# A hybrid encoder step on one core: small matmuls in another order, a rotary sum moved by DMA, decays put into copies, first weights in pieces

## What is computed

```python
hn = rmsnorm(x)
qa,ka,va,ga | qb,kb,vb,gb,low | qc,kc,vc = hn @ W_in
A = retention(rotary(qa), rotary(ka) * 1/8, va)      # 4 heads, chunks of 64, scalar decay gamma_h
B = gla(qb * 1/8, kb, vb, log_f(low))                # 4 heads, chunks of 64, decay per element
C = band_attention(qc, kc, vc)                       # 8 heads
x = x + concat[norm(A)*silu(ga), norm(B)*silu(gb), C] @ W_out
x = x + relu(rmsnorm(x) @ W_up)**2 @ W_down
```

```python
intra = (q @ k.T * decay_mask) @ v          # GLA: diagonal plus six block levels
inter = (q * q_decay) @ S                   # S: state before the chunk
S_new = chunk_decay * S + (k * k_decay).T @ v
```

## Time and profile before

| | |
|---|---|
| three runs | 1427.19, 1427.49 and 1432.36 us, median 1427.49 |
| the profiled execution | 1426.0 us, span 1424.2 us |
| PE busy | 1396.7 us (98%), 12608 matmuls |
| DVE, ACT, POOL busy | 803.9 (56%), 531.2 (37%), 144.7 us (10%) |
| 16 DMA engines, share of span | 28%, 127.70 MB at 90 GB/s |
| layer 0's slots with mixer stages, to the last `back` | from 46.3 us to 156.2 us |

### The profile page before, as it was taken

How to read it: one execution, slowest core, us unless ns; L and a number is a source line. 1 busy time by engine, 2 the same in 40 slices (tenths; PEclk the granted TensorE clock), 3 DMA queues, 4 the chain that set the end, 5 groups by cost and what they waited for, 6 DMA issues and landing times.

```text
span 1424.2 us, 28758 instructions
## 1 busy us (share of the span) xinstructions
PE 1396.7 (98%) x12608; PEld 1354.9 (95%) x12608; DVE 803.9 (56%) x1248; ACT 531.2 (37%) x885; POOL 144.7 (10%) x107
## 2 busy tenths in 40 slices
PE   7999999999999999999999999999999999999997
PEld 6999989899999999999999998989999999999996
DVE  6697866845434435335768867676453353453445
ACT  5323555733313223123333235556332231231333
POOL 0200000021020110110302000000301102102011
PEclk9999999999999999999999999999999999999999
DMA  6112333223222222222221123332232222222221
GB/s 227 61 50 90 119 95 109 76 89 95 87 79 91 87 89 89 89 89 90 92 75 46 57 93 110 97 122 75 76 103 88 83 87 87 88 90 90 89 75 64
DMA packets 60268, 127.70 MB, mean 90 GB/s; under 512 B 10864, under 2 KB 30448, under 8 KB 60144
## 3 DMA queue, kind: packets, MB, share of 16 engines
q1 hardware_dynamic: 59856, 124.82, 27.4%
q10 hardware_dynamic: 288, 1.05, 0.2%
HBM read 118.63 MB, written 7.21 MB: 88 GB/s over the span
## 4 chain that ended last, share of the span: by engine, by line
PE 90%; DVE 5%; ACT 3%; issue 2%; DMA 0%; POOLq 0%; POOL 0%; DVEq 0%; SPq 0%; ACTq 0%
PE PS L1328 87%; PE PS L1579 1%; ACT whi L486 1%; ACT Pr L613 1%; PE PS L1451 1%; DVE Pr L1102 0%; PE PS L1538 0%; DMA h<-in_x 0%; DVE wlo L809 0%; DVE F L904 0%; DVE gb L950 0%; DVE Pr L1114 0%; DVE O L892 0%; DVE gst L890 0%; DVE QK L916 0%
## 5 line engine op out<-in xcount | busy, mean ns | idle before, releaser
L809 DVE TENSOR_TENSOR wlo<-raw,whi 128x1024 fp32r<-128x1024 f32 x200 | 251.5, 1258 | 360.4 <-ACT whi L486 359.7
L486 ACT ACTIVATE whi<-raw 128x1024 fp32r<-128x1024 f32 x200 | 211.5, 1058 | 592.5 <-PE PS L1328 592.3
L1328 PE MATMUL PS<-xhi,whi 128*128 128x272 f32 x1920 | 408.0, 294 | 9.6 <-DVE wlo L809 9.5
L1328 PE MATMUL PS<-xhi,wlo 128*128 128x272 f32 x1920 | 397.6, 289 | 0.0
L1328 PE MATMUL PS<-xlo,whi 128*128 128x272 f32 x1920 | 396.4, 288 | 0.0
L1328 PEld LDWEIGHTS PS<-xhi,whi 128*128 128x128 f32 x1920 | 301.0, 189 | 21.1 <-issue 16.1
L1328 PEld LDWEIGHTS PS<-xlo,whi 128*128 128x128 f32 x1920 | 302.2, 189 | 0.0
L1328 PEld LDWEIGHTS PS<-xhi,wlo 128*128 128x128 f32 x1920 | 300.3, 189 | 0.0
L1328 PE MATMUL PS<-zhi,whi 128*128 128x272 f32 x1280 | 267.9, 288 | 0.6 <-DVE wlo L809 0.4
L1328 PE MATMUL PS<-zhi,wlo 128*128 128x272 f32 x1280 | 267.5, 288 | 0.0
L1328 PE MATMUL PS<-zlo,whi 128*128 128x272 f32 x1280 | 266.5, 288 | 0.0
(11 more groups left out here) (232 smaller groups left out, 1127.5 us busy)
## 6 DMA issues: line engine op xcount, KB each, us to landing
raw<-in_wu SPq DMA_DIRECT2D x198, 512.0 KB, 3.5
Bh<-in_bias SPq DMA_DIRECT2D x16, 256.0 KB, 3.9
h<-in_x SPq DMA_DIRECT2D x8, 272.0 KB, 6.0
out_y<-h SPq DMA_DIRECT2D x8, 272.0 KB, 2.4
ckb<-in_ck SPq DMA_DIRECT2D x8, 256.0 KB, 3.7
cvb<-in_cv SPq DMA_DIRECT2D x8, 256.0 KB, 5.5
out_k_p<-ktk SPq DMA_DIRECT2D x8, 256.0 KB, 2.4
out_v_p<-vtk SPq DMA_DIRECT2D x8, 256.0 KB, 2.4
```

What stands on the lines that cost most here:

```text
L486: nc.scalar.activation(whi[n % SPL][:, :], raw[n % RAW][:, :], ACT.Copy).then_inc(sems["w_hi"], 1)
L809: nc.vector.tensor_tensor(wlo[n % SPL][:, :], raw[n % RAW][:, :], f32(whi[n % SPL][:, :]), ALU.subtract).then_inc(sems["w_lo"], 1)
L1328: return nc.tensor.matmul(out, lhsT, rhs, start=start, stop=stop, skip_group_check=True)
```

## The change

1. `chunks` yields the two chunks of a pair for head p = 0, then the same two for p = 1: the row half changes after every two calls.
2. A `level` stage is one stretch for both heads ahead of its slot.
3. The 32 sample tokens are handled as a window of 64 tokens (the last 32 prompt tokens and the 32 sample tokens), with the same 64x64 tiles as the chunks; in a level both column halves get a copy, so that one masked copy on DVE takes 10 blocks. `Ps` is gone, `Pm` has two more blocks, and POOL clears three late parts.
4. The rotary sums are two operations on 128 partitions, and eight DMAs on SP's queue, SBUF to SBUF, put each 32 partitions at their place.
5. Retention's decays move: k's into the copies of `tok` on ACT, q's into the sum of `out` and `out_s` on DVE. The 8 scalings are gone.
6. Units 0 and 1 come in four pieces of 256 columns; ACT splits, DVE subtracts and PE waits by the piece.

```diff
+        def window(g):
+            return slice((g + 1) * T - CH, (g + 1) * T)
...
-                    def chunks(head=None):
-                        for p in range(2) if head is None else (head,):
-                            for g in range(2):
-                                for c in range(NC):
+                    def chunks():
+                        for g in range(2):
+                            for c in range(0, NC, 2):
+                                for p in range(2):
                                     yield p, g, c
+                                    yield p, g, c + 1
...
-                            for p, g, c in chunks(piece):
+                            for p, g, c in chunks():
...
                             if H <= TS // 2:
-                                for p in (piece,):
-                                    for g in range(2):
-                                        r, o = slice(64 * p, 64 * p + 64), slice(g * T + TP, (g + 1) * T)
+                                for g in range(2):
+                                    for p in range(2):
+                                        r, o = slice(64 * p, 64 * p + 64), window(g)
                                         rhs = t[r, o].rearrange("p (b x h) -> p b x h", x=2, h=H)[:, :, 1, :]
-                                        last = mm(PS[0:TS, M0 + b0 + p, 256 + 16 * g:272 + 16 * g], t[r, o], rhs)
+                                        for e in range(2):
+                                            last = mm(PS[64 * e:64 * e + 64, M0 + b0 + p, 256 + 32 * g:288 + 32 * g], t[r, o], rhs)
...
-                            if st[0] == "level" or st in MID:
-                                stage(st, 1)
+                            if st in MID:
+                                stage(st)
...
-                                pe.wait_ge(sems["rot_ready"], upto("rot_ready", 4))
+                                pe.wait_ge(sems["rot_moved"], upto("rot_moved", 16 * 16))
```

```diff
-ROTARY = {(8, 0): (RK, 0), (8, 1): (RK, 1), (10, 0): (RQ, 0), (10, 1): (RQ, 1)}
+ROTARY = {(8, 0): RK, (10, 0): RQ}
...
+                    def rotary(first):
+                        dve.wait_ge(sems["unit_read"], upto("unit_read", first + 2))
+                        nc.vector.tensor_tensor(sq[0][:, :], rot[0][:, :], sq[0][:, :], ALU.subtract)
+                        nc.vector.tensor_tensor(sq[1][:, :], rot[1][:, :], sq[1][:, :], ALU.add).then_inc(sems["rot_sum"], 1)
...
+                    def rotary_out(which):
+                        sp.wait_ge(sems["rot_sum"], upto("rot_sum", which + 1))
+                        for hd in range(4):
+                            for half in range(2):
+                                r, g = 64 * (hd % 2) + 32 * half, hd // 2
+                                sp.dma_start((rk, rq)[which][r:r + 32, g * T:(g + 1) * T], sq[half][32 * hd:32 * hd + 32, :]) \
+                                    .then_inc(sems["rot_moved"], 16)
...
                         if n == RQ:
-                            dve.wait_ge(sems["rot_ready"], upto("rot_ready", 2))
+                            dve.wait_ge(sems["rot_sum"], upto("rot_sum", 1))
+                        if n == RQ + 1:
+                            dve.wait_ge(sems["rot_moved"], upto("rot_moved", 16 * 8))
...
-                            if kind == RET:
-
-                                for t, tab, s0 in ((rk, kd_sb, CH), (rq, qd_sb, 0)):
-                                    for g in range(2):
...
+                                        ACT.Copy, scale=kd_sb[:, hd:hd + 1])
...
+                                if st[1] == RET:
+                                    for g in range(2):
+                                        ins = nc.vector.scalar_tensor_tensor(
+                                            o_v[:, g, p], src[:, g], qd_sb[:, 0, 2 * g + p:2 * g + p + 1], o_v[:, g, p],
+                                            ALU.mult, ALU.add)
```

```diff
-                        for kc in range(KC):
-                            act.wait_ge(x_in[kc], 16)
-                            xhi_tile(kc, 0)
-                            if kc < 2:
-                                split(kc)
...
+                        for k in range(PIECES):
+                            act.wait_ge(x_in[2 * k], 16)
+                            xhi_tile(2 * k, 0)
+                            for n in range(2):
+                                cols = slice(k * PIECE, (k + 1) * PIECE)
...
+                                nc.scalar.activation(whi[n][:, cols], raw[n][:, cols], ACT.Copy) \
...
+                            act.wait_ge(x_in[2 * k + 1], 16)
+                            xhi_tile(2 * k + 1, 0)
...
+                                if kc >= KC - 2:
+                                    pe.wait_ge(sems["w_lo"], n + 1)
+                                elif kc % 2 == 0:
+                                    pe.wait_ge(piece_lo, kc + n + 1)
```

More of the change, by code:

```diff
@@ L33 @@
 GROUPS = FF // D
+PIECES, PIECE = 4, D // 4
 LEVELS = [32, 16, 8, 4, 2, 1]
@@ L256, in hybrid_encoder @@
         x_in = [sem(f"x_in{kc}") for kc in range(KC)]
+        piece_in = [[sem(f"piece_in{n}{k}") for k in range(PIECES - 1)] for n in range(2)]
+        piece_hi, piece_lo = sem("piece_hi"), sem("piece_lo")
         y_done, y_scaled, y_added, y_squares, y_weighted, y_summed, y_total, y_mean, y_log, y_guess, y_rstd, y_ready = (
@@ L444, in _ @@
                 links = [0]
-                for n in range(2):
-                    act.dma_start(raw[n][:, :], wu[n, :, :]).then_inc(sems[f"w_in{n}"], 16)
+                for k in range(2):
+                    for n in range(2):
+                        first_piece(act, n, k)
                 def link(ins):
@@ L812, in _ @@
                     if layer == 0:
-                        for kc in range(KC):
-                            xlo_tile(kc, 0, upto)
-                            if kc < 2:
-                                rest(kc)
-                            else:
-                                add_square(kc - 2, upto)
+                        for k in range(PIECES):
+                            xlo_tile(2 * k, 0, upto)
+                            for n in range(2):
+                                cols = slice(k * PIECE, (k + 1) * PIECE)
+                                if k + 1 < PIECES:
+                                    dve.wait_ge(piece_hi, 2 * k + n + 1)
+                                else:
+                                    dve.wait_ge(sems["w_hi"], n + 1)
+                                nc.vector.tensor_tensor(wlo[n][:, cols], raw[n][:, cols], f32(whi[n][:, cols]), ALU.subtract) \
+                                    .then_inc(piece_lo if k + 1 < PIECES else sems["w_lo"], 1)
+                            xlo_tile(2 * k + 1, 0, upto)
+                            if k:
+                                add_square(2 * k - 2, upto)
+                                add_square(2 * k - 1, upto)
                         add_square(KC - 2, upto)
@@ L1176, in _ @@
                         if (n, half) in ROTARY:
-                            rotary(*ROTARY[(n, half)])
+                            rotary(ROTARY[(n, half)])
                         if half == 0 and n > GATE + 1:
@@ L1361, in half_products, with stage @@
                         return ins
-                    def chunks(head=None):
-                        for p in range(2) if head is None else (head,):
-                            for g in range(2):
-                                for c in range(NC):
+                    def chunks():
+                        for g in range(2):
+                            for c in range(0, NC, 2):
+                                for p in range(2):
                                     yield p, g, c
-                    def stage(st, quarter=0):
+                                    yield p, g, c + 1
+                    def stage(st):
                         what = st[0]
```

199 lines of the change are left out of this document (105 added, 94 removed).

## The result

| | before | after |
|---|---|---|
| median | 1427.7 us (1427.2 to 1432.4, 4 runs) | 1416.4 us (1415.7 to 1417.6, 4 runs) |
| profiled span | 1424.2 | 1413.5 |
| granted clock over the span | 0.998 | 0.993 |

The ratio is 0.9907, 95% interval 0.9888 to 0.9925: 11.3 us faster, where 23.0 were forecast. Of the span's 10.7 us the start gives 2.9 and each layer 3.9; a layer was to give 10.2. (PE is TensorE, DVE VectorE, ACT ScalarE, POOL GpSimd, SP SyncE; a granted clock of 1.00 is 2.4 GHz, of 0.50 is 1.2 GHz.)

What follows compares the result with a forecast made beforehand. PE was taken to bound the kernel, with 90% of the chain. Savings of 10.2 us a layer, 20.4 for both, plus 2.6 at the start made 23.0, so a median of 1404.5 us, range 1400 to 1412.

Steps and rivals of the forecast that it cites:

- Prices of the stretches: PE's added time per mixer stage: 1.23 us for 64 matmuls, 1.46 with the window, for levels, diagonals and kv.
- the pace of 29 ns: Time per small matmul in a level piece of the old order; kv's order was put at 15 to 16 ns.
- A floor of 25 ns: Rival: short matmuls in levels never start under 25 ns apart, a level costs 2.3 us, total 1418.5; chance 0.04.
- DVE becomes the bound of the level stretch: Rival: PE stalls 2 to 4 us a layer behind DVE in the level stretch, total 1410.5; chance 0.14.
- one microsecond of slack: Level stretch: PE needs 17.5 us against some 16.5 of DVE work, so DVE keeps ahead.
- PE comes 0.7 sooner and waits 0.7 longer: gain 0: Before level 0: GLA's shorter diagonal only lengthens PE's wait for DVE's last masked product, so nothing is gained.
- loss 0.2: Retention's q decay in DVE's sums for out and out_s: the smaller operations add 0.2 us to PE's path a layer.
- behind the 3.0 us of 24 products: ACT's eight k copies with decay, some 2.4 us, are hidden by products before the next transposes want the banks.
- Without that cover it would be 1.2: Cost in us a layer of ACT's k copies if the 24 products did not hide them.
- Rotary by DMA, price 0: Rotary transfers on SP land 13 to 15 us after kv, within PE's 16, so PE does not wait.
- Start 2.6: Units 0 and 1 in quarters let PE start sooner: gain 2.6 us, between 1.2 and 3.3.
- The range's lower end: 1400.5 us in the main case: x 1.3 earlier and 0.5 us a layer more from overlap; stated range from 1400.

## Why the prediction was wrong

The direction was right, the size was not: 1416.4 lies outside 1400 to 1412. The step that failed is that PE would find DVE's results ready in the shorter level stretch, with the one wait that grew, before level 0, priced at nothing. By its steps, for one layer:

- **Prices of the stretches: right in sum, wrong in parts.** A level 1.39 for 1.46, diagonal 1.45 for 1.46, kv 1.40 for 1.46; levels 0 to 3 with GLA's diagonal gained 4.9, as forecast (1.05 + 3.8). But the pace of 29 ns was mis-sized: the order gives 0.72 of a level's 1.34, the merging 0.62. `out` gave 0.76 each, not 0.9. A floor of 25 ns, that rival's condition, isn't there in levels either: 80 matmuls in 1.39 us are 17 ns each, way in and out included. The Trainium skill has that floor in "TensorE: Matmul & The Clock Gate", section "Wait — 56ns, not 53.3ns?"; by it they would take 2.0 us, and the measurement decides.
- **"DVE becomes the bound of the level stretch": the rival that came true**, at 2.8 us a layer (0.7, 0.8 and 1.4) of its 2 to 4. I gave it 0.14. The working had one microsecond of slack from DVE's busy time in the kernel before, which took over the lengths of DVE's operations unchanged. They are not constant: the shorter levels pushed DVE's operations onto POOL's, 2.1 us a layer more. DVE needed 18.5 us where I had 16.5, against the 17.5 that I gave PE: the slack was negative before any wait in the chain.
- **"PE comes 0.7 sooner and waits 0.7 longer: gain 0" before level 0.** True as far as it goes (1.15 became 2.18), but a longer wait isn't free. Behind it PE ran 3.4 us at 1.2 GHz: 1.5 us lost. This cost was in no term and no rival. With the one behind retention's `back` it is 2.6 us a layer, 4.9 measured in the whole.
- **Decays "loss 0.2": mis-sized.** I took the small operations by their share of elements; four of 0.41 and four of 0.21 make the sums 0.75 longer, and PE's wait before `back` went from 1.05 to 2.00. Since the half clock came with it, taking it back is worth 4.8 us.
- **ACT's copies "behind the 3.0 us of 24 products": wrong.** I had 2.4 us for them and counted from the transposes' end. They took 3.2, and a `whi` of 1.06, issued first, stood before them: 0.54 idle, 0.73 with its slow restart. "Without that cover it would be 1.2" bounded it.
- **Rotary by DMA, price 0: right**, with a term mis-sized. SP issued rq's eight transfers from 98.88 to 104.31, 5.4 us where I had 3.6; they landed some 2.5 us after their issue, and the retention diagonal began at 107.85 without a wait.
- **Start 2.6: within its bounds**, 2.9 in the profiled execution and 2.3 on average over twelve traces; by medians 1.7, by runs of equal clock 2.7.
- **The range's lower end does not follow from its terms.** A start of 3.3 and 0.5 us a layer more make 1402.8, not 1400.5. It didn't matter, since the miss is at the other end.

Per layer: 2.8 for DVE, 2.6 for the clock, 0.8 more idle before `back`, 0.7 for ACT's copies, 0.3 for `out` are 7.2; the score stage (1.27 for 1.57) and the fewer restarts behind pieces give back about 1. That is the 6.3 missing in each layer.

What stays open: why the same idle time is followed by the half clock in one layer or execution and not in another, behind what the kernel before loses its clock in 30 of 44 runs, and where a stop of PE for `issue` as at 832 comes from.

## What to carry to other kernels

When the engine that bounds a kernel gets faster, redo the busy account of the next one at the new spacing, meetings between DVE and POOL included: an engine at 85% of a stretch has no slack once the stretch shrinks by a fifth. Price a longer wait of TensorE above its length: look at the granted clock behind each idle stretch, in several executions, and put products ahead of the late stage, or useless ones into the wait, where it falls (here a filling of 5 was enough in two runs of five, 14 to 16 products in all five). An edit's gain alone is not its gain in company; measure the combination.

## What the runs showed of the hardware that I had not expected

- TensorE fell to 1.2 GHz for 3.4 us (twice 6.8) after 1.5 to 2.2 us without matmuls, not each time, once after 1.25, and once for 10 us around a stop of 2.81. Sixty matmuls whose results nobody reads made the kernel 4.9 us faster. After the 1.15 idle in the profiled execution of the kernel before it did not fall, but other executions of it have a lower granted clock.
- The same kernel's runs stand in steps by their granted clock, here those of the kernel before: 1425.8 to 1427.5 us at 0.998, 1427.6 to 1428.6 at 0.997, 1429.7 to 1430.2 at 0.995, 1432.3 to 1432.8 at 0.993.
- A DVE operation with two SBUF inputs took 1.87 to 2.16 us in place of 0.72 when POOL's ran, and ended 0.6 us after it each time. Splitting the level tables over the two engines saved DVE nothing.
- ACT's copy of 256 columns with a factor took 0.47 us and of 64 columns 0.31: a small operation costs two thirds of the large one's time, here 3.2 us for what plain copies do in 1.5 (v's: 1.09 and 0.38).
